# Prompt latent attention in the head space, a shorter query stage, page loads and zero-row stores placed elsewhere

## What is computed

```python
q = (rms_norm(c_q, q_norm_g) @ w_uq).reshape(B, S, N_MLA_HEADS, D_NOPE + D_ROPE)      # 8 heads, 64 + 32
q_lat = jnp.einsum('bshn,chn->bshc', q[..., :D_NOPE], w_uk)                           # c = 256 latent
q_rope = apply_rope(q[..., D_NOPE:], pos)
rows = concatenate([rms_norm(c_kv, kv_norm_g), apply_rope(k_r, pos)], axis=-1)        # 256 + 32
s = einsum('bqhc,bkc->bhqk', q_lat, ckv) + einsum('bqhr,bkr->bhqk', q_rope, krope)
p = softmax(where(k_pos <= q_pos, s * MLA_SCALE, -inf))
o_lat = einsum('bhqk,bkc->bqhc', p, ckv)
o_mla = einsum('bshc,chv->bshv', o_lat, w_uv)                                         # v = 64
```

## Time and profile before

| what | us |
|---|---|
| median of three timed runs (2845.81, 2848.34, 2850.04) | 2848.34 |
| the profiled execution's own time | 2838.72 |
| its span, first to last instruction | 2836.9 |

### The profile page before, as it was taken

One profiled execution on the slowest core, in us unless ns is written; L12 is line 12 of the kernel. 1 busy time (PEld: TensorE's weight loads), 2 busy tenths in 40 slices (PEclk: granted clock), 3 DMA queues, 4 the chain that ended last, 5 costly groups with the idle time before them and its releaser, 6 DMA issues. The chain is left out here.

```text
span 2836.9 us, 40591 instructions
## 1 busy us (share of the span) xinstructions
PE 2623.5 (92%) x16201; PEld 2174.7 (77%) x16201; DVE 1442.9 (51%) x3440; ACT 351.4 (12%) x1020; POOL 673.5 (24%) x678
## 2 busy tenths in 40 slices
PE   7879996689899999999999999888999999999997
PEld 4555363344559999999999967454899999999997
DVE  1431003002238997997555322113599799955553
ACT  2311012001212112110000010011211111100000
POOL 0154200000001332444333100000033244443330
PEclk8899998789999999999999999999999999999999
DMA  4697978988561998999999998569169999999995
GB/s 143 220 370 239 316 253 303 408 333 295 239 251 56 389 390 293 352 372 337 409 409 409 343 338 311 196 226 399 64 254 379 339 329 343 347 399 409 409 409 197
DMA packets 249865, 885.13 MB, mean 312 GB/s; under 512 B 31802, under 2 KB 39130, under 8 KB 238879
## 3 DMA queue, kind: packets, MB, share of 16 engines
q1 hardware_dynamic: 165630, 591.13, 56.0%
q0 software_dynamic: 84048, 291.41, 27.1%
HBM read 863.08 MB, written 109.08 MB: 343 GB/s over the span
## 5 line engine op out<-in xcount | busy, mean ns | idle before, releaser
L2652 PE MATMUL ps<-xT,front 128*128 128x192 f32 x4096 | 686.0, 326 | 8.2 <-DMA front<-in_peer_uT 6.8
L2652 PEld LDWEIGHTS ps<-xT,front 128*128 128x128 f32 x4096 | 663.2, 190 | 12.8 <-DMA front<-in_peer_uT 9.9
L2678 PE MATMUL ps<-p1e_S,p_qT 128*128 128x192 f32 x2048 | 337.1, 327 | 6.3 <-DMA p_qT<-in_peer_v 6.3
L2678 PE MATMUL ps<-p0e_S,p_qT 128*128 128x192 f32 x2048 | 336.9, 327 | 4.9 <-DMA p_qT<-in_peer_v 4.9
L2678 PEld LDWEIGHTS ps<-p1e_S,p_qT 128*128 128x128 f32 x2048 | 332.4, 190 | 10.8 <-DMA p_qT<-in_peer_v 10.5
L2678 PEld LDWEIGHTS ps<-p0e_S,p_qT 128*128 128x128 f32 x2048 | 332.4, 190 | 9.1 <-DMA p_qT<-in_peer_v 9.0
L2430 DVE CUSTOM_DVE_ANT_0 front<-front,x_tok 128x1024 f32<-128x1024 f32 x256 | 309.9, 1219 | 7.6 <-DMA front<-in_peer_u,p0e_expert 2.7
L2331 POOL DMA_INDIRECT front<-in_peer_u,p0e_expert x128 | 153.1, 1196 | 387.4 <-DVE p0e_dots L2430 206.0
L2331 POOL DMA_INDIRECT front<-in_peer_u,p1e_expert x128 | 153.1, 1196 | 386.5 <-DVE p1e_dots L2430 204.8
L2441 DVE SCALAR_TENSOR_TENSOR h_tok<-front,p1e_dots,h_tok 128x1024 f32<-128x1024 f32 x127 | 163.1, 1285 | 141.5 <-DMA front<-in_peer_v,p1e_expert 140.7
L2441 DVE SCALAR_TENSOR_TENSOR h_tok<-front,p0e_dots,h_tok 128x1024 f32<-128x1024 f32 x127 | 163.2, 1285 | 141.5 <-DMA front<-in_peer_v,p0e_expert 140.6
(11 more groups left out here) (480 smaller groups left out, 3077.4 us busy)
## 6 DMA issues: line engine op xcount, KB each, us to landing
front<-in_peer_uT SPq DMA_DIRECT2D x256, 512.0 KB, 6.9
p_qT<-in_peer_v SPq DMA_DIRECT2D x256, 512.0 KB, 7.3
out_swa_sample<-in_cache_swa_w SPq DMA_DIRECT2D x32, 2040.0 KB, 22.1
e_ring<-in_swa_kT SPq DMA_DIRECT2D x16, 1024.0 KB, 9.0
e_arena<-in_swa_v SPq DMA_DIRECT2D x16, 1024.0 KB, 13.8
out_swa_sample<-in_cache_swa_w SPq DMA_DIRECT2D x8, 2016.0 KB, 31.5
...
```

Of the source, the lines that this page charges most:

```text
L2652: mm = pe.matmul(k.ps[:, SB[i % len(SB)], 0:TD], ur[:, i % NU, c, :], k.xT[:, c, D0:T], start=(c == 0), stop=(c == KC - 1))
L2678: mm = pe.matmul(k.ps[:, c // 2, c % 2 * TD:(c % 2 + 1) * TD], vr[:, i % NV, c * P:(c + 1) * P], S[:, i, :], start=False, stop=(i == STEPS ...
```

## The change

- **Queries and keys.** `query_stage` makes, for all tokens, two groups of four heads' rotary features as full 128-column tiles (weights laid out on the host, `mla_w_q`), the unrotated features as 128-column tiles of two heads (`qnT`), then keys (`knT`) and values (`vp`) of the 256 prompt tokens in the head space, and latent queries for the 64 sample tokens only. DVE rotates four heads at once and spreads the samples' rotary queries with 16 copies; `krT` is kept four times over, on 128 partitions.
- **Prompt attention.** `mla_prompt` is its own stage with 8 units, a pair of heads and a block of queries each: scores with 64 and 32 rows of contraction, values of 64 columns written directly to `oT` by ACT. `mla_values_stage` is left with the 64 sample tokens.
- **SP's lists.** The eight copies of window rows go to the first projection stage; mask, `w_uv`, page table and bias inputs are loaded in `latent_stage`, which no longer waits for the stored rows (the query stage does) but waits for the loads. Parts 0 to 3 are asked for in the query stage (POOL gathers part 5 there), parts 4 and 6 and the 16 zero-row stores stay in the prompt attention. The four key loads go from "swp" to "kturn".
- **Buffers.** `e_ring` is allocated sooner and lends the first projection its room; five part slots are a buffer of their own; the mask has its own buffer.

The diff, cut; of `query_stage`, whose removed lines stand above, added lines only. The new functions `load_table`, `load_early` and `load_later` hold the old `first_loads` in three pieces.

```diff
-PARTS_AHEAD, GATHERED_AHEAD = (0, 1, 2, 3, 4, 6), (5,)
+PARTS_EARLY, PARTS_LATER, GATHERED_AHEAD = (0, 1, 2, 3), (4, 6), (5,)
...
-        return pieces[:DEC_B] + zero_rows + pieces[DEC_B:]
+        return pieces, zero_rows
...
+    def store_zero_rows(self, eng):
...
+            eng.dma_start(dst, src).then_inc(self.copied, 16)
...
+        sp.dma_start(self.wq[:, :, :], io["mla_w_q"].rearrange("(c p) n -> p c n", p=P)).then_inc(k.query_landed, 16)
+        sp.dma_start(self.csT[:, :, :], io["rope_feat"]).then_inc(k.query_landed, 16)
...
-            sp.dma_start(self.wsw[:, c, :, 0:16], uq[:, c, :, NOPE + 16:NOPE + 32]).then_inc(k.query_landed, 16)
-            sp.dma_start(self.wsw[:, c, :, 16:32], uq[:, c, :, NOPE:NOPE + 16]).then_inc(k.query_landed, 16)
...
+        sp.dma_start(self.e["wuv"][:, :, :, :],
+                     io["mla_w_uv"][0].rearrange("(c p) h n -> p c h n", p=P)).then_inc(k.query_landed, 16)
+        sp.dma_start(self.e["mask"][:, :, :], io["causal"]).then_inc(k.query_landed, 16)
...
             weights.load(sp)
+            pages.load_table(sp)
+            bias.load(sp)
+            sp.wait_ge(k.query_landed, weights.due)
             sp.wait_ge(rows_ready, 3)
...
+            sp.dma_start(io["mla_rows_sample"][0].rearrange("b s c -> (b s) c"), rows[0:64, 2, :]).then_inc(k.query_landed, 16)
         @block.scalar
...
+                dve.tensor_copy(rope4[0:n, i], rows[0:n, i, 256:288].unsqueeze(1).to_broadcast([n, 4, ROPE])).then_inc(rows_ready, 1)
...
+            pages.load_early(sp)
+            sp.wait_ge(k.query_landed, weights.due + 32)
...
+            pe.wait_ge(k.query_landed, weights.due)
+            for g in range(2):
+                for v in range(2):
+                    c0 = n_nope + n_rope * v + P * g
+                    for c in range(2):
+                        mm = pe.matmul(k.ps[:, 4 + 2 * g + v, 0:T], wq[:, c, c0:c0 + P], cqT[:, c, :], start=(c == 0), stop=(c == 1))
+                mm.then_inc(rope_made, 1)
...
+                    mm = pe.matmul(k.ps[:, pair, 0:T], wq[:, c, pair * P:(pair + 1) * P], cqT[:, c, :], start=(c == 0), stop=(c == 1))
+                mm.then_inc(nope_made, 1)
...
+                pe.wait_ge(rope_taken, half + 1)
+                for i in range(2):
+                    for c in range(2):
+                        pair = 2 * half + i
+                        mm = pe.transpose(k.ps[:, 4 + 2 * half, (2 * i + c) * P:(2 * i + c + 1) * P],
+                                          wuk[:, c, pair * P:(pair + 1) * P], k.ident[:, :])
+                mm.then_inc(uk_turned, 1)
...
+                pe.wait_ge(nope_taken, pair + 1)
                 for c in range(2):
+                    mm = pe.matmul(k.ps[:, pair, 0:SEQ], wuk[:, c, pair * P:(pair + 1) * P], ckvT[:, c, 0:SEQ],
+                                   start=(c == 0), stop=(c == 1))
+                mm.then_inc(key_made, 1)
...
+            for c in range(2):
+                pe.wait_ge(uk_taken, 2)
+                for pair in range(4):
+                    for half in range(2):
+                        rows = slice(64 * half, 64 * half + 64)
+                        mm = pe.matmul(k.ps[:, 4 + 2 * c + half, pair * 64:pair * 64 + 64], wukT[rows, pair, c * P:(c + 1) * P],
+                                       e["qnT"][rows, pair, SEQ:T], start=True, stop=True)
+                mm.then_inc(lat_made, 1)
+            for kb in range(2):
+                pe.wait_ge(key_taken, kb + 1)
+                for c in range(2):
+                    mm = pe.matmul(k.ps[:, kb, 0:MLA_H * D_V], ckvT[:, c, kb * P:(kb + 1) * P],
+                                   wuv[:, c].rearrange("p h n -> p (h n)"), start=(c == 0), stop=(c == 1))
+                mm.then_inc(value_made, 1)
...
+            pages.find_rows(pool)
...
+                    last = dve.tensor_tensor(out=rot[:, v, :], in0=k.ps[:, 4 + 2 * g + v, 0:T], in1=csT[:, v, :], op=ALU.mult)
...
+            for a in range(4):
+                src = e["qr"][ROPE * a:ROPE * (a + 1), :, SEQ:T].rearrange("p g (u s) -> p u g s", u=DEC_B)
+                for part in range(4):
+                    rows = e["qrp"][ROPE * part:ROPE * (part + 1), :, part, :].rearrange("p u (g a s) -> p a u g s", g=2, a=4)
+                    dve.tensor_copy(rows[:, a], src)
+            for c in range(2):
+                dve.wait_ge(lat_made, c + 1)
+                for half in range(2):
+                    dst = pages.q[:, c].rearrange("p u (a e) s -> p e a u s", e=2)
+                    dve.tensor_copy(dst[:, half], k.ps[:, 4 + 2 * c + half, 0:256].rearrange("p (a u s) -> p a u s", a=4, u=DEC_B))
...
+                for c in range(2):
+                    for half in range(2):
+                        mm = pe.matmul(k.ps[64 * half:64 * half + 64, half, pair * n:(pair + 1) * n], wuv[:, c, 2 * pair + half, :],
                                        e["olatT"][:, c, 2 * pair + half, :], start=(c == 0), stop=(c == 1))
...
+        return [n for n in range(len(self.chunks)) if 1 + n == u]
...
+    def load(self, sp):
...
+        sp.dma_start(self.rel[:, :], io["rel_fill"]).then_inc(k.bias_landed, 16)
+        sp.dma_start(self.hot[:, :], io["bucket_hot"]).then_inc(k.bias_landed, 16)
+        sp.wait_ge(k.bias_landed, 32)
...
+            sp.dma_start(self.rel[r0:r0 + N_BUCKETS, own], io["rel_bias"][:, own]).then_inc(k.bias_landed, 16)
...
             pages = LatentPages(k, c1, e)
-            mla_prompt(k, e, pages)
+            with ExitStack() as cb:
+                bias = BiasByDistance(k, cb)
+                with ExitStack() as c2:
+                    e["cqT"] = k.sb(c2, "e_cqT", [P, 2, T])
+                    e["latent"] = k.sb(c2, "e_latent", [P, 3, first])
...
+                    preload_window_keys(k, sp, room)
+                    sp.wait_ge(k.bias_tabled, BiasTables.count)
...
+        units = [(qb, pair) for qb in range(2) for pair in range(MLA_H // 2)]
...
+        def _(sp):
+            pages.load_later(sp)
+            k.store_zero_rows(sp)
...
+                for half in range(2):
+                    rows = slice(64 * half, 64 * half + 64)
+                    pe.matmul(k.ps[:, 2 * (u % 2) + half, 0:n], e["qnT"][rows, pair, qs], e["knT"][rows, pair, 0:n],
+                              start=True, stop=False)
+                for half in range(2):
+                    h = 2 * pair + half
+                    rows = slice(ROPE * (h % 4), ROPE * (h % 4) + ROPE)
+                    mm = pe.matmul(k.ps[:, 2 * (u % 2) + half, 0:n], e["qr"][rows, h // 4, qs], e["krT"][rows, 0:n],
+                                   start=False, stop=True)
+                mm.then_inc(scored, 1)
...
+                nk = keys(u) // P
+                pe.wait_ge(p_ready, u + 1)
+                wait(pe, pT_ready, u - 1)
+                for half in range(2):
+                    for kb in range(nk):
+                        j = half * nk + kb
+                        mm = pe.transpose(k.ps[:, 4 + u % 2, j * P:(j + 1) * P], p[:, u % 2, half, kb * P:(kb + 1) * P], k.ident[:, :])
+                mm.then_inc(turned, 1)
...
+                pe.wait_ge(pT_ready, u + 1)
+                wait(pe, bias.taken, len([n for v in range(u + 1) for n in bias.of_unit(v)]))
+                for kb in range(nk):
+                    for half in range(2):
+                        h = 2 * pair + half
+                        mm = pe.matmul(k.ps[64 * half:64 * half + 64, 6 + u % 2, 0:P],
+                                       e["vp"][:, kb, D_V * h:D_V * (h + 1)], pT[:, u % 2, half * nk + kb, :],
+                                       start=kb == 0, stop=kb == nk - 1)
+                mm.then_inc(o_ready, 1)
...
+            scores(0)
+            scores(1)
+            for u in range(U):
+                if u > 0:
+                    values(u - 1)
+                turn(u)
+                wait(pe, o_taken, u - 1)
+                bias.tensor(pe, u)
+                if u + 2 < U:
+                    scores(u + 2)
+            values(U - 1)
...
+                dve.tensor_tensor(out=dst, in0=score_banks(u), in1=e["mask"][:, units[u][0], 0:n].unsqueeze(1).to_broadcast([P, 2, n]),
+                                  op=ALU.add).then_inc(s_read, 1)
+                dve.wait_ge(s_read, u + 1)
+                link(dve.reduce_max(stat[:, u % 2, 0, :], dst, AX))
...
+                                  op0=ALU.mult).then_inc(max_ready, 1)
...
+                    last = dve.tensor_scalar(out=p[:, u % 2, half, 0:n], in0=p[:, u % 2, half, 0:n],
+                                             scalar1=stat[:, u % 2, 3, half:half + 1], scalar2=None, op0=ALU.mult)
+                last.then_inc(p_ready, 1)
...
+            for u in range(U):
+                finish(u)
+                if u + 1 < U:
+                    maxima(u + 1)
...
+                for half in range(2):
+                    last = act.activation(p[:, u % 2, half, 0:n], s[:, u % 2, half, 0:n], ACT.Exp,
```

(22 more changed lines are left out.)

316 lines of the change are left out of this document (152 added, 164 removed).

## The result

The changed kernel takes 2814.9 us (median of 4 runs, 2813.8 to 2817.9), the kernel before beside it 2847.1 (4 runs, 2844.7 to 2850.0). The ratio is 0.9890, interval 0.9874 to 0.9905: 32 us less, where I forecast 47. The profiled executions are only 23.8 apart (spans 2836.9 and 2813.1), and the stages of the table make all of it. The two last columns were taken later on a second chip, which takes longer for the sample attention in either kernel.

The account below looks back on a forecast made before the run. It took PE, with DVE and ACT, to bound most early stages, SP's list the 16 idle us, and the DMA the windowed samples. 4.2 - 13.6 - 29.6 - 3.0 - 2.5 - 3.0 = -47.5 us gave 2801, range 2787 to 2815.

Parts of the forecast that it names:

- Prompt attention: Prompt attention stage: eight units of a pair of heads each shorten it from 66.6 to 37.0 us, -29.6.
- the units: Prompt attention: DVE and ACT chain sets 3.0 or 3.9 us a unit; with a bias product 4.4 or 5.0.
- The rival of the low clock: Latent stage ends at 55, queries take 3 more, bias units at their upper end: +11 us, 2812; chance 0.18.
- 'PE will be idler': Prompt attention: reason for taking 4.4 and 5.0 us for bias units, the stretch having stood at 0.83 of the clock.
- Latent stage: Latent stage: SP waits for 4.0 MB of loads at 330 GB/s, so it ends at 51.2 instead of 47.0, +4.2 us.
- Query stage: Query stage: 18.9 us of PE work plus half clock, waits and barrier; from 37.0 to 23.4 us, -13.6.
- Sample attention: Sample attention: 2.8 us pause before the third sample goes, the table's spreading partly takes its place; -3.0 us.
- window projection at nothing: Window projection, behind the values stage: no change in time, 0.
- Windowed samples: Windowed sample attention, bound by the DMA: window keys moved earlier save -3.0 us, between 0 and -6.
- First projection at nothing: First projection: eight added copies, 3.9 MB, cost nothing, the DMA being 17% busy there.
- Changes of tile shape: Prompt attention: 32 shape changes stall PE; at 1.8 us each 2859, slower than before; rival's chance 0.015.
- 'Something else, not seen here, holds the barriers': Stage barriers: something unseen holds them and nothing is gained, within 0.2%; rival's chance 0.015.

Follow-up runs that it names:

- spread_in_sample: Changed kernel with POOL spreading the bias table in the sample attention instead of the prompt attention: prompt attention 39.1 us, sample attention 140.6.
- copies_alone: As spread_in_sample, but POOL also issues four 2.0 MB cache copies in the prompt attention: that stage took 61.8 us, POOL last by 23 us.
- before_zero_later: Kernel before without its 16 zero-row stores in the prompt attention: that stage took 54.0 us instead of 67.7.
- bias_after_exp: Changed kernel with ACT copying the bias product after the next unit's exponentials: ACT done 40.3 us into the prompt attention, as in the changed kernel.
- no_bias: Changed kernel with SP spreading the table, repetitions outermost, and the five bias products left out: engines done 34.0 us into the prompt attention, stage ended at 37.9.
- filler: As spread_in_sample, with useless PE products in the prompt attention and values stages: prompt attention 31.1 us, against 38.9 in samp_hot on the same chip.
- after: The changed kernel itself, in its first profile: 2814.9 us against 2847.1 for the kernel before, ratio 0.9890.
- after_again: The changed kernel run once more, unaltered, on the second chip: 2852.9 us against 2881.7 for the kernel before, ratio 0.9903.
- keys_back: Changed kernel with window keys asked for where the kernel before did, behind the windowed prompt attention's stores: windowed sample attention 138.6 us instead of 135.6.
- samp_hot: As spread_in_sample, with bias inputs asked for at the head of the query stage: 2808.0 us against 2845.6 for the kernel before, ratio 0.9871.
- spread_one: Changed kernel with two of the three table spreads issued by SP, one by POOL: engines done at 114.8, next stage began at 131.1.
- best_tail: Changed kernel with late bias inputs, prompt-attention filler, and POOL's rows-outermost spread behind its last sample-attention gather: 2784.1 us against 2846.1, ratio 0.9796.

## Why the prediction was wrong, step by step

The sign was right, and queries, samples, values and keys came within 2 us. The prompt attention was mis-sized by 17 us, which is more than the 15 by which the medians miss the forecast.

- *Prompt attention, -29.6 forecast, -12.4 measured.* Two terms failed. First, **the end of the stage**: the prediction asked whether SP's list or the engines end it and named POOL's spread only as traffic for the next stage. POOL's rows of before were there, its queue coming to an end at 144.8 beneath SP's zero rows; I had not asked of POOL what I asked of SP:
```profile
111.12 0.56 POOL L1385 DMA_DIRECT2D scratch_bias_by_dist<-bs_by_dist  x1 [8.90 <-ACT bs_by_dist L1415]
114.59 3.34 POOL L1389 DMA_DIRECT2D scratch_bias_rep<-scratch_bias_by_dist  x3 [2.91 <-DMA scratch_bias_by_dist<-bs_by_dist]
150.53 0.10 POOL L1722 MEMSET ms_mask<- 64x8 f32 x1 [32.60 <-POOLq L165]
```
It cost 12.9 us (131.9 instead of 119.0), shown by spread_in_sample, copies_alone and before_zero_later. Second, **the units**: for the bias units 4.4 and 5.0 us were taken, 4.7 and 5.2 to 5.8 measured, and the engines were done at 40.9 us instead of 36.6. The text says "PE itself has under 2.7 us of work in a unit" and so charged the half clock to the bias product alone; at half clock PE had 4.7 to 5.8 us of work in such a unit and was the bound (bias_after_exp, no_bias, filler). The rival of the low clock, 2812, comes near the measured total by luck: its 3.9 us for the bias units are the 4.3 measured, but of its 7 us of late loads and slow queries less than 2 came, and it has no POOL. 'PE will be idler' holds for the gap before the clock fell, not for what followed: there PE was busy at half clock until its last two units.
- *Latent stage, +4.2 forecast, +5.8 measured.* Right mechanism; the term mis-sized is the rate. 4.0 MB from SP's first issue took 15.4 us until `bs_hot` had landed, 260 GB/s where 330 was taken: for the first 4 us the loads are small, SP issues one each 0.5 us and the DMA moves under 200 GB/s. In the last 4 us `bs_hot` moves nearly alone, 239 GB/s with the DMA 67% busy, near the eleven engines of sixteen that the prediction names beside this wait.
- *Query stage, -13.6 forecast, -15.1 measured* (-14.3 on the second chip). PE dense as said, half clock for its first 4.5 us (6.2 on the second chip), SP hidden by 2.3 us.
- *Sample attention, -3.0 forecast, -2.0 measured* (-4.6 on the second chip). The 2.8 us pause before the third sample is gone (152.45); a new one of 0.8 stands inside the second sample (143.33). The spread, which the prediction let take part of the gain, was over before the stage began.
- *Values, -2.5 forecast, -2.7 measured*, but the **window projection at nothing was wrong** in most profiles: +2.4 in after and after_again, where the clock fell at the values stage, 0 in keys_back, samp_hot and spread_one, where it was full again by the projection. In the kernel before it never fell there. Where it falls, the values stage's gain is gone.
- *Windowed samples, -3.0 forecast, -3.0 measured*, cause shown by keys_back.
- *First projection at nothing.* Right for the copies: with the same code there the stage took 21.0 us in about half of the profiles and 22.5 to 24.0 in the others, by how long PE's first products ran at the slow interval. The kernel before had 21.0 in all three of its profiles, which may be chance.
- *Profile against median.* I let the 9.6 us between them stand. All behind the windowed samples took 2239.0 us in the profile of before and 2238.9 in that of after, so the profiles' difference lies in the stages of the table. The two long stages of 860 us varied from 859.9 to 865.9 and 857.7 to 867.9 us with the same code, and the profile of before is at the low end. That and the first projection's 3 us can make the 8 between 23.8 and 32; it was not separated further.
- *Rivals.* SP's list did not end the stage (done 29.9 us into it). Changes of tile shape cost nothing that can be seen: at the full clock (78.04 to 79.72 of after) groups of two 128-column products, 64 rows and 32 rows in turn, follow each other by 0.42 us, and by the prediction's 1.67 ns a column two such products are 0.43. The DMA took nothing back. 'Something else, not seen here, holds the barriers', given 0.015, is what happened in one stage.

Open: why the clock came back after 17, 27 or 55 us; why this chip or that reads the pages at 230 or at 300 GB/s; and how much of samp_hot's 15 us is the order in POOL's queue and how much the four-engine form of the spread; the two were changed together in best_tail.
